# A transformer kernel on one core: the products of the identity with itself around the norms are left out

## The reference

```
# first block
h = rms_norm(x, norm_mix_pre);  proj = h @ w_in
x = x + rms_norm(merged @ w_out, norm_mix_post)        # merged: stick-breaking attention and a gated convolution
h = rms_norm(x, norm_ffn_pre);  u = causal_dwconv(h @ w_up)
x = x + rms_norm((gelu(g) * a) @ w_down, norm_ffn_post)
# second block
u = rmsnorm(x, norm_mix_g);     proj = u @ w_in_2      # gated delta rule and forgetting attention
h = x + merged @ w_out_2
hn = rmsnorm(h, norm_mlp_g)
x = h + square(relu(hn @ w_up_2)) @ w_down_2
```

## Time and profile before

| | us |
|---|---|
| median of three runs | 1022.8 |
| the profiled execution, whole | 1023.85 |
| its span, first to last instruction | 1022.1 |
| PE busy | 998.6 |
| DVE busy | 579.4 |
| ACT busy | 508.6 |
| POOL busy | 211.2 |

### The profile page before, as it was taken

The page is one execution under the profiler, slowest core; times in us unless marked ns, Lnnn a source line. Parts: engine busy times, 40 slices in busy tenths (PEclk is TensorE's granted clock), DMA queues, the critical chain, the costliest instruction groups (busy, mean ns, idle before and its releaser), DMA issues.

```text
span 1022.1 us, 19129 instructions
## 1 busy us (share of the span) xinstructions
PE 998.6 (98%) x8131; PEld 975.0 (95%) x8131; DVE 579.4 (57%) x835; ACT 508.6 (50%) x776; POOL 211.2 (21%) x206
## 2 busy tenths in 40 slices
PE   7999998999999999999999989999999999999998
PEld 7999998989999998999999989999899999999998
DVE  5456456377777645666256785552456655454442
ACT  5375854465555543565455752323354445554331
POOL 6001002311111001246333672221100001110000
PEclk8999999999999999999999999999999999999999
DMA  8643445365555554355325323112255545565550
GB/s 272 208 145 104 159 159 191 112 198 198 165 193 169 194 188 129 119 165 165 124 83 165 124 84 124 44 45 79 83 160 171 171 141 184 171 200 186 186 191 16
DMA packets 151448, 152.47 MB, mean 149 GB/s; under 512 B 5169, under 2 KB 150852, under 8 KB 151364
## 3 DMA queue, kind: packets, MB, share of 16 engines
q1 hardware_dynamic: 151348, 151.25, 45.9%
q10 hardware_dynamic: 16, 0.00, 0.0%
HBM read 150.20 MB, written 1.05 MB: 148 GB/s over the span
## 4 chain that ended last, share of the span: by engine, by line
PE 86%; DVE 7%; ACT 3%; POOL 2%; issue 1%; DMA 1%; SPq 0%; POOLq 0%; DVEq 0%; ACTq 0%
PE ps L1725 74%; PE ps L1693 6%; PE ps L1912 4%; PE ps L1690 2%; DVE wl L753 2%; DMA raw<-in_w_in 1%; DVE gv L780 1%; ACT wh L1258 1%; POOL rs L528 1%; DVE mt L1157 1%; ACT xs L1292 0%; POOL fg L597 0%; PE ps L1892 0%; DVE xres L780 0%; DVE tA L1019 0%
## 5 line engine op out<-in xcount | busy, mean ns | idle before, releaser
L753 DVE TENSOR_TENSOR wl<-raw,wh 128x1024 fp32r<-128x1024 f32 (+2 forms) x261 | 309.1, 1199 | 210.1 <-ACT wh L1258 210.0
L1725 PE MATMUL ps<-xh,wh 128*128 128x256 f32 x1280 | 369.8, 289 | 2.9 <-ACT wh L1258 2.9
L1725 PE MATMUL ps<-xh,wl 128*128 128x256 f32 x1280 | 363.4, 284 | 0.9 <-DVE wl L753 0.9
L1725 PE MATMUL ps<-xl,wh 128*128 128x256 f32 x1280 | 359.6, 284 | 0.0
L1258 ACT ACTIVATE wh<-raw 128x1024 fp32r<-128x1024 f32 (+2 forms) x292 | 287.1, 1022 | 107.5 <-PE ps L1725 106.0
L1725 PEld LDWEIGHTS ps<-xh,wh 128*128 128x128 f32 x1280 | 246.3, 192 | 7.2 <-ACT wh L1258 3.2
L1725 PEld LDWEIGHTS ps<-xh,wl 128*128 128x128 f32 x1280 | 246.3, 192 | 1.1 <-DVE wl L753 1.1
L1725 PEld LDWEIGHTS ps<-xl,wh 128*128 128x128 f32 x1280 | 244.7, 193 | 0.0
L536 POOL TENSOR_TENSOR wl<-raw,wh 128x1024 fp32r<-128x1024 f32 (+1 forms) x31 | 77.7, 2507 | 140.6 <-ACT wh L1258 139.1
L1725 PE MATMUL ps<-wh,xh 128*128 128x256 f32 x288 | 84.3, 294 | 4.3 <-ACT xh L1281 4.3
L1725 PE MATMUL ps<-wl,xh 128*128 128x256 f32 x288 | 82.0, 286 | 0.0
(11 more groups left out here) (337 smaller groups left out, 1594.5 us busy)
## 6 DMA issues: line engine op xcount, KB each, us to landing
raw<-in_w_in SPq DMA_DIRECT2D x56, 1024.0 KB, 5.0
raw<-in_w_up SPq DMA_DIRECT2D x38, 1024.0 KB, 5.1
raw<-in_w_down SPq DMA_DIRECT2D x24, 1024.0 KB, 5.0
raw<-in_w_out SPq DMA_DIRECT2D x8, 1024.0 KB, 4.9
raw<-in_w_proj_fox SPq DMA_DIRECT2D x4, 1024.0 KB, 5.0
raw<-in_w_proj_gdn SPq DMA_DIRECT2D x4, 1024.0 KB, 4.9
raw<-in_w_down SPq DMA_DIRECT2D x4, 768.0 KB, 4.8
raw<-in_w_conv_branch SPq DMA_DIRECT2D x4, 512.0 KB, 3.4
```

The costliest lines, as they stand in the source:

```text
L753: e.tensor_tensor(WL[v][:, k:kc, :], RAW[s][:, k:kc, :], WH[v][:, k:kc, :].bitcast(F32), ALU.subtract).then_inc(lo.sem)
L1725: k = e.matmul(o, l, r, start=first and n == 0, stop=done and n == 3 * kc - 1, skip_group_check=not (first and done))
```

## The change

The table `WARM`, the function `warm` and all its calls are removed. Everything else stands as it was, with the line numbers moved up by a few (1690 becomes 1689, 1725 becomes 1724). 60 products go: 12 at the start, and 16 at each of norms 1, 2 and 3.

```
--- before.py
+++ after.py
@@ -24,7 +24,6 @@
 NW = 3
 AHEAD = 2
 MAIN = 3
-WARM = (12, 4, 12)
 POOL_HALF = frozenset([*range(26, 33), *range(74, 98)])
 LATE_LO = frozenset([33, 67])
 CHAIN_AT = ((8, 36), (11, 36), (18, 36), (21, 39))
@@ -1732,15 +1731,9 @@
                                 begins()
                             side.tick()
 
-            def warm(n):
-                for _ in range(n):
-                    mul(PS[7][:, 0:P], ident[:], ident[:])
-
 
             def norm(n, bank=None):
                 for a in range(2):
-                    if a and n:
-                        warm(WARM[1])
                     for c in range(8):
                         b, j = 3 + c // 2, c % 2
                         if c in (0, 4):
@@ -2007,7 +2000,6 @@
 
 
             e.wait_ge(*cst("id"))
-            warm(WARM[2])
             e.wait_ge(ld_r, 16)
             e.transpose(PS[7][:, 0:8], R1[0:8, :], ident[0:8, 0:8]).then_inc(gn.sem)
             norm(0)
@@ -2029,13 +2021,11 @@
                 unit(U_YA + i, oH, oL, lambda q: att_act[1]("oh", q), lambda q: att_dve[1]("ol", q))
             for i in range(4):
                 unit(U_WO + i, XH, XL, lambda q: ymh("hi", q // 2), lambda q: ymd("lo", q // 2), fresh=i == 0)
-            warm(WARM[0])
             norm(1)
             for v in range(FC1):
                 unit(U_UP + v, XH, XL, **(x_of(1) if v == 0 else {}))
             for u in range(U_DN, U_FQ):
                 unit(u, fH, fL, lambda q: fhi("hi", q // 2), lambda q: flo("lo", q // 2))
-            warm(WARM[0])
             norm(2)
             side.add(small())
             for n in range(8):
```

## The result

The changed kernel takes 1025.04 us (median of 15 runs, 1023.16 to 1026.34), the kernel before 1022.3 us (15 runs, 1021.47 to 1023.83). The ratio is 1.0022 with a 95% interval of 1.0014 to 1.0030: slower by 2.25 us, 1.4 to 3.1. (The medians lie 2.74 us apart, the means 2.2; the text goes by the ratio.) Forecast was slower by 4.8 us. The time lies in the range given, near its lower end, the way was right, and the size was twice too large.

The account below looks back on a forecast made before the run. TensorE, busy 98% of the span, was taken as the bound. Clock falls at three norms, 3 x 1.6 = +4.8 us, with start 0 and removed time 0, gave 1027.6 us; range of 8 in 10: 1024.3 to 1030.4 us.

Parts of the forecast that it names:

- The removed time is worth nothing: 60 products, about 16.5 us of busy TensorE, priced at 0 because the norms' chain of ACT, DVE and POOL hides them.
- The clock falls in all three norms: TensorE's clock drops to half in norms 1, 2 and 3, 1.6 us each, +4.8 us; chance 0.60.
- Rival 1: Norm 3 keeps its clock, its longest gap being 2.3 us; two norms pay, 3.2 us, 1026.0 us; chance 0.20.
- The price of time at half clock: Per norm: second eight turns 0.8 us longer, 43% of later half-clock time lost, less 0.9 us slack.
- R - S: Time at a norm from the second eight turns' start (S) to the clock's return (R); 3.9 to 7.8 us expected.
- How long the half clock holds behind the second eight turns: At each norm, back 3.9 to 6.1 us after S or S + 1.7; costs 0.85 to 2.5 us, 1.6 taken.
- Norm 2 comes out alike: Norm 2 has less slack, 24 products of the small projection following, but was priced like the others at 1.6 us.
- The start, 0: Leaving out the 12 products at the start was priced at 0, with bounds of -0.95 and +0.3 us.
- Rival 3: Faster: at the start the first product comes 0.7 us earlier and the clock returns sooner; 1.6 us, 1021.2 us; chance 0.04.
- Rival 2: The clock holds everywhere, through all norms: no change, 1022.8 us; chance 0.10.
- rival 4: Longer cold: half clock lasts beyond 6.1 us or one more fall comes; 10 us, 1031 to 1033 us; chance 0.06.
- The sign for a wrong size: Falls present, but second turns' start to third group of products grows by under 0.85 or over 2.5 us per norm.

Follow-up runs that it names:

- e2: The products of norms 1, 2 and 3 left out of the kernel before, the 12 at the start kept: ratio 1.0019, +1.9 us.
- e10: The changed kernel run once more with a profile, nothing altered: 1024.2 us, one run.
- e4: Against the kernel before, only the 12 products ahead of norms 1, 2 and 3 left out, the 4 in the middle and the start's 12 kept: ratio 1.0019.
- e12: Against the kernel before, 6 products in place of 12 ahead of norms 1, 2 and 3, the rest kept: ratio 1.0013, +1.3 us.
- e5: Against the kernel before, each product of the identity replaced by two turns of the identity at the same places: ratio 1.0004.
- e9: The changed kernel run once more with a profile, nothing altered: 1025.6 us, one run.
- e1: Against the kernel before, only the 12 products ahead of norm 0, at the start, left out: ratio 1.0001, 1022.76 against 1022.27 us.

## Why the prediction was right in its way and wrong in its size

*The removed time is worth nothing.* Right: 6.64 us of chain before and 6.63 after, 11.2 us less busy time and nothing gained.

*The clock falls in all three norms.* Right, in all five profiles without products at the norms. The comparison of the gaps of 4.35, 4.49 and 2.3 us with the 2.05 us of 609.80 held. Rival 1 (norm 3 keeps its clock; it is the forecast by the Trainium skill, TensorE: Matmul & The Clock Gate, Why this matters for your kernels) did not come up: at norm 3, with 2.21 us idle, the clock fell each time, in e2 and e10 only behind the second idle piece of 1.47 us. With the 4 products left in the middle it held in one profile (e4). But e12 held behind 3.01 us, so the length of a gap alone is a weak guide in either direction.

*The price of time at half clock.* Right: 0.8 + 0.43 x (R - S - 1.7) - 0.9 gives the delays to 0.15 us in 13 of the 15 falls. Only its R - S was wrong.

*How long the half clock holds behind the second eight turns.* This is the step that failed, and it carries the whole error. I set "back after 3.9 us" to 6.1, counted from S, and added another 1.7 us for the case that turns don't count; the value taken, 1.6 us a norm, stands for R - S of about 5.7 us. Measured: 2.16 to 5.32, mean 3.95, 0.79 us a norm. What was wrong is the point that the length was counted from. The 3.9 to 6.1 us of the earlier trace rows run from the start of dense work, and there the clock had fallen just before or just behind that start: at 13.0 for work at 13.66, at 176.9 for 177.72, at 610.4 for 609.80. In a norm it is mostly down long before S, and the stretch from fall to return is no longer for that: 6.8 us in 13 of 15, as in two of the three of the kernel before. At norm 2 of the changed profile it fell at 404.2 and was back at 411.0; 3.9 us of the stretch lie ahead of the second turns (408.10), where TensorE waits for DVE anyway or does its first eight turns without holding anything up, and 2.9 us behind them. For the upper bound the turns were also taken as no work for the clock. The runs contradict that (e5, e10); by how much the turns shorten a stretch isn't shown. Three norms at 0.79 us are 2.4 us, against 1.9 (e2) and 2.25 us (the change) in the timed runs.

*Norm 2 comes out alike.* Wrong in four of five profiles, where norm 2 pays 0.29 to 0.45 us, the least of the three. In e9 it is norm 1 that pays 0.25 and norm 2 that pays 1.03. So it follows when the clock falls, and not the slack of the norm.

*The start, 0.* Right in its timed size (e1: 1.0001). The profile alone would have misled: it has -1.05 us there, from weights that happened to land earlier and a clock that was back at 18.5 instead of 19.8. Rival 3 (faster by the start) falls with e1. Rival 2 (clock holds everywhere) falls with every profile of the changed kernel, rival 4 (longer cold) with R - S never over 5.32.

*The fall at 610* is gone in the changed profile and present in the one before, and moves the paired products by 1.6 us, which are given back by 616: TensorE then waits for DVE's gv. That fall costs nothing.

*The bounds and the signs.* That the time lies in the range is partly luck. The delay by the ratio, 2.25 us, is less than the sum's own lower bound for three falls, 3 x 0.85 = 2.55 us; the range reached lower by the 0.95 us of the start, which e1 doesn't show. (That bound is 1022.8 + 2.55 - 0.95 = 1024.4, and not the 1024.5 of the prediction.) The sign for a wrong size came up: norms 2 and 3 of the changed profile are later by 0.45 and 0.84 us, under 0.85. R - S of norm 2, 2.92 us, lies below the 3.9 to 7.8 us that were to be seen. And the 15 us of waiting for DVE's xs at the later norms are 10.9 us (15.3 in all, 4.4 of them at the start), with 2.2 us at norm 3 put down to DVE's xres.

## What to carry to other kernels

Work that nobody uses can be worth its place on TensorE where the engine waits several times for a few microseconds: left out it gains nothing, and the clock at half costs 43% of the time that it holds into dense work, less the slack there. To price a fall, take the length of a stretch at half clock from its fall to its return (6.8 us here, at times 3.4) and count only the part behind the start of dense work; the part that lies in the wait is free. Then look for the gaps that have no such fill yet, which here were worth more (3.6 us) than the fills in question (2.25 us). Don't put fills ahead of late work unless the clock is sure to be up: at half clock 4 of them take 1.92 us, at full clock 1.06 (e4, norms 1 and 3), and they stand in the way.

## What I had not expected of the hardware

Turns with the identity hold the granted clock (e5, ratio 1.0004) and can raise it (e5 at its start, and e10: a product of 0.39 us behind 16 turns alone, in one of five executions). An idle piece of 2.86 us let the clock fall at one norm, and one of 3.01 us at another didn't (e12). In the norms the stretch at half clock lasted 6.8 us (13 times) or 3.4 us (twice), while the moment of the fall moved against the same work by over 3 us. So R - S went from 2.16 to 5.32, which is why profiles of one kernel differ by 1 us at each norm.
